# Gated attention in a decoder layer: state product per head on 64 rows, head outputs in two PSUM banks, and a VectorE update that waits for ScalarE's copy

## What is computed

```python
def step(state, inp):
    q_, k_, v_, a_ = inp
    b = jnp.cumsum(a_, axis=2)
    o_inter = jnp.einsum('bhck,bhkv->bhcv', q_ * jnp.exp(b), state)
    ...
    scores = jnp.einsum('bhik,bhjk,bhijk->bhij', q_, k_, decay)
    o_intra = jnp.einsum('bhij,bhjv->bhiv', scores, v_)
    b_last = b[:, :, -1:, :]
    k_dec = k_ * jnp.exp(b_last - b)
    state = (jnp.exp(b_last[:, :, 0, :])[..., None] * state
             + jnp.einsum('bhck,bhcv->bhkv', k_dec, v_))
    return state, o_inter + o_intra
```

## Time and profile before

| | us |
|---|---|
| median of 3 runs | 2063.23 (2062.63 to 2064.51) |
| the profiled execution, its own time | 2063.08 |
| span of the profiled execution | 2061.3 |
| TensorE matmuls busy | 2043.2 (99%) |
| VectorE busy | 1422.8 (69%) |
| ScalarE busy | 981.5 (48%) |

### The profile page before, as it was taken

How to read it: one execution, slowest core, us unless ns; L and a number is a source line. 1 busy time by engine, 2 the same in 40 slices (tenths; PEclk the granted TensorE clock), 3 DMA queues, 4 the chain that set the end, 5 groups by cost and what they waited for, 6 DMA issues and landing times.

```text
span 2061.3 us, 29111 instructions
## 1 busy us (share of the span) xinstructions
PE 2043.2 (99%) x11424; PEld 1680.0 (82%) x11424; DVE 1422.8 (69%) x2131; ACT 981.5 (48%) x1323; POOL 222.9 (11%) x391
## 2 busy tenths in 40 slices
PE   9999999999999999999999999999999999999998
PEld 8778788778778878888888788888788888888887
DVE  6687668656866688766657766766666668766477
ACT  5454544454445447655546545444433334433333
POOL 3000000000000013245301121111100000000000
PEclk9999999999999999999999999999999999999999
DMA  6143252425142525467665786776978657766564
GB/s 188 53 122 114 71 168 59 134 62 173 53 123 62 178 71 162 138 220 221 198 225 203 250 320 246 276 275 240 340 230 272 194 194 226 243 194 191 194 219 164
DMA packets 244329, 374.36 MB, mean 182 GB/s; under 512 B 18032, under 2 KB 119504, under 8 KB 244192
## 3 DMA queue, kind: packets, MB, share of 16 engines
q1 hardware_dynamic: 213536, 275.82, 41.3%
q0 software_dynamic: 30656, 96.67, 14.0%
HBM read 272.81 MB, written 99.61 MB: 181 GB/s over the span
## 4 chain that ended last, share of the span: by engine, by line
PE 88%; DVE 7%; DMA 2%; ACT 1%; issue 1%; POOL 0%; DVEq 0%; ACTq 0%; POOLq 0%
PE main L69 17%; PE main L71 17%; PE main L70 17%; PE sc L69 7%; PE sc L70 7%; PE sc L71 7%; PE aux L71 1%; PE aux L70 1%; PE ob L69 1%; PE ob L70 1%; PE aux L69 1%; PE ob L71 1%; PE sc L552 1%; DVE xpT L1223 1%; DVE q_lev L1170 1%
## 5 line engine op out<-in xcount | busy, mean ns | idle before, releaser
L1781 DVE TENSOR_TENSOR w_lo<-w_b,w_hi 128x1024 fp32r<-128x1024 f32 x142 | 173.5, 1223 | 162.6 <-ACT w_hi L1748 162.2
L1748 ACT ACTIVATE w_hi<-raw 128x1024 fp32r<-128x1024 f32 x142 | 150.1, 1059 | 224.6 <-PE main L71 95.2
L1781 DVE TENSOR_TENSOR w_lo<-raw,w_hi 128x1024 fp32r<-128x1024 f32 x142 | 173.6, 1223 | 104.1 <-ACT w_hi L1748 103.9
L1748 ACT ACTIVATE w_hi<-w_b 128x1024 fp32r<-128x1024 f32 x142 | 150.0, 1057 | 158.2 <-PE aux L71 77.2
L69 PE MATMUL main<-xT_lo,w_hi 128*128 128x512 f32 x512 | 210.5, 411 | 0.0
L71 PE MATMUL main<-xT_hi,w_hi 128*128 128x512 f32 x512 | 200.1, 391 | 0.0
L70 PE MATMUL main<-xT_hi,w_lo 128*128 128x512 f32 x512 | 199.8, 390 | 0.0
L1137 DVE TENSOR_TENSOR w_lo<-raw,w_hi 128x1024 fp32r<-128x1024 f32 x114 | 138.6, 1221 | 70.3 <-ACT w_hi L811 68.6
L69 PE MATMUL sc<-x_lo,w_hi 128*128 128x512 f32 x448 | 174.5, 389 | 1.3 <-DVE z L2198 1.3
L69 PE MATMUL main<-x_lo,w_hi 128*128 128x512 f32 x448 | 174.4, 389 | 0.0
L70 PE MATMUL sc<-x_hi,w_lo 128*128 128x512 f32 x448 | 174.3, 389 | 0.0
(11 more groups left out here) (306 smaller groups left out, 4500.6 us busy)
## 6 DMA issues: line engine op xcount, KB each, us to landing
raw<-in_w_in_dram SPq DMA_DIRECT2D x80, 512.0 KB, 3.8
h_dram<-z SPq DMA_DIRECT2D x64, 512.0 KB, 3.8
raw<-h_dram SPq DMA_DIRECT2D x112, 256.0 KB, 2.7
w_b<-h_dram SPq DMA_DIRECT2D x112, 256.0 KB, 2.7
h_dram<-h_s SPq DMA_DIRECT2D x48, 512.0 KB, 3.6
raw<-in_w_out_dram SPq DMA_DIRECT2D x32, 512.0 KB, 3.5
raw<-in_w_ff_dram SPq DMA_DIRECT2D x32, 512.0 KB, 6.3
w_b<-in_w_ff_dram SPq DMA_DIRECT2D x32, 512.0 KB, 5.1
```

Source lines behind the costliest of these rows:

```text
L1748: act.activation(hi, slot_tile(ff, m), ACT.Copy).then_inc(ff.hi_done, 1)
L1781: dve.tensor_tensor(lo, slot_tile(ff, m), hi.bitcast(F32), ALU.subtract).then_inc(ff.lo_done, 1)
```

## The change

In `attend` the two k_dec products come first. The output of head 0 stays in `ob`; that of head 1 goes to columns 256 to 383 of the `aux` bank. The two `probs` products follow, and then the two state products, each on the 64 rows of its own head in `state` and `q_dec`. `ob_done` now comes with head 0's state product and `aux_done` with head 1's, the last product of the call. `copy_o` waits for both and copies in two instructions of 128 columns, the second of which gives `ob_free`. `update_state` also waits for that `ob_free`, because what it releases, `aux`, now also holds head 1's output.

```diff
@@ attend
+                place = (ob[:, 0:CH], aux[:, 256:256 + CH])
+                for e in range(2):
+                    pe.matmul(aux[64 * e:64 * e + 64, 0:DV], k_dec_rows[:, c, 64 * e:64 * e + 64],
+                              v_rows[:, c, DV * (2 * hp + e):DV * (2 * hp + e) + DV], start=True, stop=True)
                 for e in range(2):
                     vh = v_rows[:, c, DV * (2 * hp + e):DV * (2 * hp + e) + DV]
-                    pe.matmul(ob[:, DV * e:DV * e + CH], vh, probs[:, CH * e:CH * e + CH], start=True, stop=False)
-                    ins = pe.matmul(ob[:, DV * e:DV * e + CH], state[:, hp, e, :], q_dec[:, tok],
-                                    start=False, stop=True)
-                ins.then_inc(ob_done, 1)
+                    pe.matmul(place[e], vh, probs[:, CH * e:CH * e + CH], start=True, stop=False)
                 for e in range(2):
-                    ins = pe.matmul(aux[64 * e:64 * e + 64, 0:DV], k_dec_rows[:, c, 64 * e:64 * e + 64],
-                                    v_rows[:, c, DV * (2 * hp + e):DV * (2 * hp + e) + DV], start=True, stop=True)
-                ins.then_inc(aux_done, 1)
+                    head = slice(64 * e, 64 * e + 64)
+                    pe.matmul(place[e], state[head, hp, e, :], q_dec[head, tok], start=False, stop=True
+                              ).then_inc((ob_done, aux_done)[e], 1)
@@ copy_o
-                act.activation(oT[:, :, CH * c:CH * c + CH], ob[:, 0:2 * CH].rearrange("p (e n) -> p e n", e=2),
-                               ACT.Copy).then_inc(ob_free, 1)
+                act.wait_ge(aux_done, AUX_USES * t + AUX_GLA + AUX_PAIR * hp + 1 + c + 1)
+                act.activation(oT[:, 0, CH * c:CH * c + CH], ob[:, 0:CH], ACT.Copy)
+                act.activation(oT[:, 1, CH * c:CH * c + CH], aux[:, 256:256 + CH], ACT.Copy).then_inc(ob_free, 1)
@@ update_state
                 dve.wait_ge(aux_done, AUX_USES * t + AUX_GLA + AUX_PAIR * hp + 1 + c + 1)
+                dve.wait_ge(ob_free, OB_USES * t + OB_GLA + 4 * hp + c + 1)
```

## The result

The changed kernel takes 2072.94 us (median of 4 runs, 2072.28 to 2074.07) against 2063.87 us for the kernel before (4 runs, 2062.63 to 2065.07). The ratio is 1.0044, 95% interval 1.0032 to 1.0056: slower by 9.1 us. The forecast was 6.6 us slower, with a range of 2065.5 to 2074.0 that holds the result. It lies in the upper part, 0.4 us beyond the 2072.5 that the forecast gave itself and inside the 2072 to 2076 of rival 1, and it is held against a median of the kernel before that came out 0.6 us above the one the forecast started from.

A forecast was written before the change was run, and what follows sets the result against it. TensorE, busy 99% of the span, was taken as the bound, with VectorE's chain setting pair ends; 1.62 + 0.92 + 4.08 = 6.6 us more gave 2069.8 us, range 2065.5 to 2074.0.

The forecast's parts named there:

- rival 1: Dearer: heads one after the other, full-price copies or waits falling out badly; 2072 to 2076 us, chance 0.15.
- TensorE's list: Each `attend` call, last column product to next scores: 1.76 us instead of 1.58, so 0.18 more.
- rival 2: 64-row state products run into the next 64x64 scores without a drain, 0.22 saved per call; 2065.3 us, chance 0.12.
- the prediction's 0.22 each: State products in `attend`: two side-by-side passes, 0.22 after a mode change plus 0.20 to the next mode, 0.42 us.
- ScalarE's copies: `copy_o`: two copies of 128 columns, 0.27 us each, overlapping by 0.11, take 0.43 us together.
- the hand-offs: Steps from TensorE to ScalarE and from ScalarE to VectorE before the update: 0.05 us each.
- The late update of `(1, 0)`: Second pairs: the update waits for ScalarE's copy, which stands behind a high part; 1.13 us later.
- First pairs: Pair ends 0.54 us later in the first, third and fourth blocks, 0.92 in the second.
- Second pairs: Pair ends 1.02 us later in each of four blocks, 4.08 in all, through late updates and masks.
- `attend(1, 2)` would start 0.75 late: Second pairs: 0.57 late from `attend(1, 1)`, plus 0.09 for the rest of the call and 0.09 for the entry.
- fourth rival: No difference: room counted as used up exists, such as another order of masks' short stalls; 2063 us, chance 0.10.
- The faster rival: TensorE's list sets the time throughout; the row pair saves 0.22 in each of 32 calls, 2056.2 us, chance 0.05.

The follow-up runs named there:

- Experiment 3: The changed kernel with its state products on all 128 rows again: 2071.88 us against 2062.93 for the kernel before.
- Experiment 8: The changed kernel with the k_dec products last, copies waiting for both signals: 2071.47 us against 2064.98 for the kernel before.
- experiment 2: The kernel before with the k_dec products first and the update waiting for the output product, one copy: 2066.36 us against 2062.93.
- Experiments 1 and 7: 1: kernel before plus two copies and VectorE's wait for the second, 2067.17 us against 2062.93; 7: that with two ScalarE copies moved forward, 2065.71 against 2064.98.
- experiment 4: The kernel before with 32 already met wait instructions added on VectorE, one per state update: 2062.05 us against 2062.93.
- experiment 9: The changed kernel with 74 already met waits ahead of VectorE's program: 2075.41 us against 2063.38 for the kernel before.
- Experiment 6: The changed kernel with two ScalarE copies moved ahead of a high part and a split: 2069.89 us against 2064.98 for the kernel before.

## Why the prediction was right, and where its size was off

**TensorE's list: right.** 1.75 us measured, 1.76 forecast; each piece came out as its row had it. The paired state products take 0.21 from first to second and 0.20 to the next mode, so rival 2 (the step to the 64x64 scores is free) is out. Experiment 3 shows the balance: with its change of mode, the pair takes as long as the four full passes that it replaces. How that divides into a saving and a price is not shown by it, since the two come together in every kernel here. What stands for the prediction's 0.22 each are the 64-row passes of L598 in the trace of before, another form (256 columns): the inner ones start 0.12 apart, the first is followed after 0.22 and the last after 0.20.

```profile
460.87 0.28 PE L598 MATMUL sc<-mkT,xqT 64*128 64x256 f32 x2
460.99 0.28 PE L598 MATMUL sc<-mkT,xq_low 64*128 64x256 f32 x2
```

Experiment 8 shows that the other 0.2 us of the list comes from putting the k_dec products first, not from the 64 rows. The Trainium skill, TensorEngine Tiling (Array Packing), Key Properties, has the rule that a change of mode drains TensorE, and the lists agree with it: for the same products 1.58 us with two changes of mode (before) and 1.78 with three (experiment 2), 1.55 with three (experiment 8) and 1.75 with four (the changed kernel). Its Theoretical Speedup of up to 2x shows in no list: the two state products take 0.42 us where the four full passes took 0.44.

**ScalarE's copies: right, the hand-offs too small.** The second starts 0.16 after the first and takes 0.27, 0.43 together. But the update comes 575.61 - 573.43 = 2.18 us after the call's first product, where the prediction added up 2.05: it took 0.05 us from TensorE to ScalarE and 0.05 from ScalarE to VectorE, and they are 0.13 and 0.10, with the last pass ending 0.02 sooner. This 0.13 us goes into the end of every pair.

**The late update of `(1, 0)`: right.** Forecast 1.13 us later, against the calls around it; measured 561.90 - 555.49 - 5.24 = 1.17 (5.24 is how late the pair began), 1.10 of it as idle time where there was none. Experiments 1 and 7 show the price of the two late copies: with ScalarE's order repaired, 4.2 us become 0.7, and 4.5 in the pairs become 2.1.

**First pairs: near, by luck.** 0.49, 0.35 and 0.36 against 0.54, and 1.19 against 0.92 in the second block. Two misses cancel. In experiment 4 the first, third and fourth first pairs were 0.18, 0.30 and 0.32 us shorter only by the pauses that left them, which the prediction counted nowhere; and the hand-offs add 0.13. So 0.54 - 0.18 + 0.13 = 0.49 and 0.54 - 0.30 + 0.13 = 0.37. The second block's pair had no pause to lose (0.08 in experiment 4), and 0.92 + 0.08 + 0.13 = 1.13.

**Second pairs: the mis-sized term.** 1.02 each was forecast, 4.08 in all, and 1.56, 1.20, 1.21 and 1.81 were measured, 5.8. The step that failed is that `attend(1, 2)` would start 0.75 late, without a wait of its own. TensorE waited there in every block. In the third block it started 573.43 - 567.06 = 6.37 late where the pair had begun 5.24 late, so 1.13. The masks of that chunk held a pause of VectorE, 0.37 us beyond the usual step, which the trace of before has at other places and which the prediction named only in its fourth rival, as room. The change's extra instructions move it: experiment 4 shows that they alone do. In experiment 9, where the pause is hidden, the same call starts 0.78 late and does not wait, which is the forecast's step, and each second pair is 0.33 to 0.38 us shorter.

The 1.4 us that experiment 9 takes from the four second pairs is not the same as what they exceed the forecast by. In the second and third blocks the kernel before pays for a pause too, one chunk later; there VectorE loses 0.37 us at one place and gets 0.35 back at the other. What the runs show for a second pair is the forecast's 1.02, with 0.13 for the hand-offs and 0.05 for the later update of `(1, 0)`: 1.20, as in the second and third blocks. In the first the pause is new, and 1.20 + 0.36 = 1.56. In the fourth it is new as well, and one mask instruction of the fourth chunk takes 0.55 us where 0.29 is usual, which gives the rest of the 1.81. It does so in experiment 9 too, but not in experiment 3, whose pair has 1.5; why stays open.

**Sum.** 8.2 us in the pairs and 9.1 by the medians. The remaining 0.9 us lies within what the medians of 4 runs leave open, an interval of 6.6 to 11.6 us by the ratio; no part of it is pinned to a cause. The same interval reaches down to the forecast's 6.6, so it is the pairs, not the medians, that show the terms to be too small. The faster rival asked for an update of `(1, 0)` less than 0.56 us late and for free changes of mode. Experiment 6 brought the first near (0.63 us of wait), the second is out by every list shown, and no kernel with the paired products was as fast as before.

## What to carry to other kernels

Packing small products on part of the array is worth counting with the steps into and out of the mode: here two state products on 64 rows took 0.42 us with their steps, where the full array took 0.44, so group products by mode before counting what packing saves. A wait of one engine for another cost most where the releaser's own list had put something else first (4.5 us in the pairs, 2.1 with the copies moved forward), so when adding one, move the releaser's instruction forward too. And look for the instruction at which the end of a stage is really set: moving a few short VectorE instructions from before the masks and updates that TensorE waits for to behind them was worth 4 us without touching TensorE. When two traces are compared, look for what has moved between them without being part of the change: here pauses on instruction numbers made some pairs look cheaper and others dearer than the change made them.

## What the runs showed of the hardware

- VectorE paused between masks, by 0.46 to 0.47 us of idle time where 0.10 is usual, at instructions 319, 703, 959, 1087, 1343 and 1471 of its list (counted from 0, waits included). All are one less than an odd multiple of 64. At one less than an even multiple (639 and 1023 in the trace of before) masks had the usual 0.10, and at 191, also an odd one, the mask started only 0.26 us later than usual. The same numbers came back in kernels with the same count of instructions, whatever they waited for, and with 20 or 37 wait instructions added ahead of them the same numbers fell on work that stands as many instructions earlier: with 20 on other masks, which had the pause, with 37 on an update that waits 1.10 us for ScalarE anyway, whose wait grew by nothing. That it has to do with how instructions are supplied was not shown.
- Two wait instructions in a row made one in the trace: 40 waits became 20 instructions, 74 became 37. VectorE's first work came 2.6 us later with the 20 and 4.3 us later with the 37.
- After TensorE's wait of 2.1 us in the feed-forward part the granted TensorE clock was 0.68 over the next 5 us, with products 0.43 us apart instead of 0.23. The profile of before waited 1.3 us at the same place and kept 1.00, but so did that of experiment 1, which waited 2.2 us there. At a later wait, around 1475 us, experiment 8 waited 2.3 us and had 0.57 in the next stretch (1474 to 1478), and experiment 9 waited 2.2 us and kept 1.00. So the length of the wait alone does not tell which it will be.
